# Two output projections that keep finished rows on chip, and four loads and stores in other places

## What is computed

```python
def layer_output(x, branches, w_out):          # end of each layer
    mixed = jnp.concatenate(branches, axis=-1) # branches, each times silu(gate)
    return x + mixed @ w_out                   # output projection and residual
# layer 0: dilated attention and retention, layer_output, giving x1
# layer 1: rmsnorm(x1) @ w_in (2864 columns), sparse attention, layer_output, giving x2
# result:  rmsnorm(x2) * final gain, for the prompt and for the samples
```

## Time and profile before

| what | value |
|---|---|
| three runs | 2055.37, 2053.42 and 2056.6 us, median 2055.37 |
| the profiled execution | 2053.46 us, span 2051.2 us, mean granted clock of TensorE 0.966 |
| PE | 1893.7 us busy, 92% of the span, 13566 matmuls |
| PE's weight load | 1455.8 us, 71% |
| DVE, ACT, POOL | 855.3, 699.1 and 507.2 us: 42%, 34%, 25% |
| DMA | 261.58 MB, mean 128 GB/s |
| chain that ended last | from 1910.78 us; DMA 2%, PE 2% and DVE 1% of the span |

### The profile page before, as it was taken

How to read it: one execution, slowest core, us unless ns; L and a number is a source line. 1 busy time by engine, 2 the same in 40 slices (tenths; PEclk the granted TensorE clock), 3 DMA queues, 4 the chain that set the end, 5 groups by cost and what they waited for, 6 DMA issues and landing times. The chain is left out here.

```text
span 2051.2 us, 35233 instructions
## 1 busy us (share of the span) xinstructions
PE 1893.7 (92%) x13566; PEld 1455.8 (71%) x13566; DVE 855.3 (42%) x2503; ACT 699.1 (34%) x1527; POOL 507.2 (25%) x628
## 2 busy tenths in 40 slices
PE   7999998997895898999969999999899999999695
PEld 6777776676663887878867555554688887888695
DVE  5222221774443424221411221212677777777433
ACT  5100000663332223000002322232577767667412
POOL 0000000796542000000004212110365555555000
PEclk9999999998996999999989999999999999999998
DMA  5444432655577754644336241332400000000565
GB/s 204 154 141 146 143 140 93 194 162 155 181 224 206 253 190 133 209 144 156 114 76 246 82 165 47 140 98 59 119 23 22 15 15 22 23 12 32 185 198 181
DMA packets 163171, 261.58 MB, mean 128 GB/s; under 512 B 33890, under 2 KB 113440, under 8 KB 158656
## 3 DMA queue, kind: packets, MB, share of 16 engines
q1 hardware_dynamic: 144976, 212.73, 32.7%
q0 software_dynamic: 4608, 33.56, 4.5%
q10 hardware_dynamic: 13424, 13.05, 2.5%
HBM read 210.57 MB, written 55.77 MB: 130 GB/s over the span
## 5 line engine op out<-in xcount | busy, mean ns | idle before, releaser
L1619 POOL TENSOR_SCALAR sparse_pr<-sparse_pr,sparse_coef,sparse_gate 128x63 f32<-128x63 f32 (+8 forms) x384 | 246.0, 658 | 208.0 <-DVE sparse_coef L1575 208.0
L1001 PE MATMUL x_acc<-x_w_hi,x_y_lo 128*128 128x478 f32 (+3 forms) x768 | 274.7, 358 | 1.9 <-DVE x_y_lo L855 1.6
L1001 PE MATMUL x_acc<-x_w_lo,x_y_hi 128*128 128x478 f32 (+3 forms) x768 | 269.2, 351 | 0.0
L1001 PE MATMUL x_acc<-x_w_hi,x_y_hi 128*128 128x478 f32 (+3 forms) x768 | 268.6, 350 | 0.0
L2656 PE MATMUL ss_ps_h<-ss_xT,cmp_w 128*128 128x508 f32 x512 | 244.0, 594 | 0.8 <-ACT ss_xT L2494 0.8
L1520 ACT ACTIVATE sparse_pr<-sparse_pr,sparse_nmax 128x63 f32<-128x63 f32 (+8 forms) x384 | 227.4, 597 | 2.7 <-DVE sparse_nmax L1569 2.7
L1621 POOL TENSOR_SCALAR dilated_pr<-dilated_pr,dilated_coef 128x1024 f32<-128x1024 f32 (+7 forms) x64 | 109.0, 1722 | 372.3 <-DVE dilated_coef L1575 372.3
L445 PE MATMUL h_acc<-h_w_hi,h_y_lo 128*128 128x512 f32 x448 | 177.3, 396 | 0.8 <-DVE h_y_lo L370 0.8
L445 PE MATMUL h_acc<-h_w_hi,h_y_hi 128*128 128x512 f32 x448 | 174.7, 390 | 0.0
L445 PE MATMUL h_acc<-h_w_lo,h_y_hi 128*128 128x512 f32 x448 | 174.6, 390 | 0.0
L1001 PEld LDWEIGHTS x_acc<-x_w_hi,x_y_lo 128*128 128x128 f32 x768 | 146.0, 190 | 29.4 <-issue 14.7
(11 more groups left out here) (353 smaller groups left out, 2780.5 us busy)
## 6 DMA issues: line engine op xcount, KB each, us to landing
h<-h_out SPq DMA_DIRECT2D x56, 256.0 KB, 2.1
h_w_side<-in_even_w_in SPq DMA_DIRECT2D x16, 896.0 KB, 5.0
h_w_raw<-in_even_w_in SPq DMA_DIRECT2D x6, 2048.0 KB, 8.0
x_w_side<-in_odd_w_in SPq DMA_DIRECT2D x16, 716.0 KB, 4.8
x_w_raw<-in_odd_w_in SPq DMA_DIRECT2D x5, 1912.0 KB, 8.5
h<-x_out SPq DMA_DIRECT2D x40, 239.0 KB, 2.2
ev_unit<-in_cache_a_k SPq DMA_DIRECT2D x4, 2048.0 KB, 8.9
ev_unit<-in_cache_a_v SPq DMA_DIRECT2D x4, 2048.0 KB, 11.1
```

The costliest lines, as they stand in the source:

```text
L1001: last = nc.tensor.matmul(acc[b][:, 0:passes[p][3]], left[:, k, t * P:(t + 1) * P], weights(right, p)[:, k, :], start=(k == 0 and a == 0), ...
L1619: nc.gpsimd.tensor_scalar(row, row, one, gate[:, t, 2 * i + e, (br + 1) % 3:(br + 1) % 3 + 1], ALU.mult, ALU.mult).then_inc(scaled, 1)
```

## The change

- **Rows kept.** In both projections the products of passes 0 and 1 of some tiles stay in SBUF (`held`): all eight tiles in the last projection, tiles 0 to 3 in the first. They are neither stored nor read back; the last 340 columns are added to the same row. In the first projection their whole rows (512 KB) are stored once, when complete. The memory comes from tiles that are idle then: `cmp_w1` in the first, keys, pieces and raw constants of the sparse phase in the last. `cmp_lent` (16 KB a partition) now serves in turn as raw weights of the first projection, the prompt's keys and values, the samples' turned keys, the prompt's turned keys, and gain, side outputs and a scratch row of the last projection.
- **Squares** of the last projection go to a scratch row; the wait for the store of the tile two before moves from ACT's square to DVE's scaling.
- **Samples of the last projection.** All eight side steps run in pass 1, one a tile. Their rows are read back at the start of the third pass, squared after tile 3, scaled after tile 4 and stored at tile 5.
- **Last quad.** The sixteen stores move from the end of `rest_of_even` into the first projection's pass 0, four behind the load of each of tiles 2 to 5; SP waits for them ahead of the samples' rows.
- **Prompt's keys and values** for the MLP are loaded on SP at the start of the first projection's last pass instead of on ACT in the sample phase.
- **Page table.** Constants are loaded first, then half the table on SP and half on ACT.
- Two phases become one, and a third (`rounds`) encloses them: one more barrier at the very end.

```diff
-    step_at = {NT + 2 * s: s for s in range(KD)}
+    step_at = {NT + (2 if norm_to is None else 1) * s: s for s in range(KD)}
...
-        w_raw = sb("w_raw", [P, KD, widest]) if early is None else early.w_raw
+        if early is None:
+            w_raw = comp.lent[:, 0:KD * widest].rearrange("p (k c) -> p k c", k=KD)
+        else:
+            w_raw = early.w_raw
...
+            held = [comp.w1[0][:, 4 * t:4 * t + 4, :].rearrange("p l f -> p (l f)") for t in range(4)]
...
+            w_side, outb, res, held, junk = early.w_side, None, early.res, early.held, early.junk
...
+        def leaves(n):
+            return n // NT > last_out or n // NT < last_out and n % NT >= len(held)
+
         def stored_count(p, t):
-            return 16 * evacuations(number(p, t))
+            n = number(p, t)
+            return 16 * sum(1 for m in range(n + 1) if m % 3 == n % 3 and leaves(m))
+
+        def kept_count(t):
+            return 16 * sum(1 for m in range(len(held), t + 1) if m % 2 == t % 2)
+
+        def row_of(t):
+            return held[t] if t < len(held) else x[:, t % 2, :]
...
-                    if t < 2:
+                    if t < len(held):
+                        return
+                    if t - 2 < len(held):
                         sp.wait_ge(turned[0], NT // 2 + 1)
                         sp.wait_ge(turned[1], NT // 2)
                     else:
                         rb, ru = turn_of(t - 2, True)
                         sp.wait_ge(rows_ready[rb], ru + 1)
-                        if norm_to is None:
-                            sp.wait_ge(completed_stored[b], 16 * (t // 2))
+                        sp.wait_ge(completed_stored[b], 16 * (t // 2))
                     for p in range(last_out):
...
+                    if not leaves(number(p, t)):
+                        return
...
-                    sp.dma_start(dst[0][place(t), KEPT:D], x[:, t % 2, KEPT:D]).then_inc(completed_stored[t % 2], 16)
+                    c0 = 0 if t < len(held) else KEPT
+                    sp.dma_start(dst[0][place(t), c0:D], row_of(t)[:, c0:D]).then_inc(completed_stored[t % 2], 16)
...
+                    if quad is not None and t == NT:
+                        quad.wait_stored(sp)
                     load_gated(t, n)
+                    if quad is not None and t < 6:
+                        quad.store_last(sp, t - 2)
...
-                        load_kept(0)
-                        load_kept(1)
+                        for t in range(len(held), min(len(held) + 2, NT)):
+                            load_kept(t)
+                        if norm_to is not None:
+                            load_sample_rows()
                     if p == first_next:
                         load_sample_rows()
                     if p == first_next + 1 and comp is not None:
                         load_compressor()
+                    if p == n_passes - 1 and comp is not None:
+                        sp.wait_ge(w_cut, n_passes - 1)
+                        for pp in range(first_next, n_passes - 1):
+                            if columns(pp).start < VC + P and KC < columns(pp).stop:
+                                for t in range(NT):
+                                    sp.wait_ge(stored[out_buffer(pp, t)[0]], stored_count(pp, t))
+                        comp.load_prompt(sp, dst_next[0])
...
+                        if p == last_out and norm_to is not None and t == 5:
+                            sp.wait_ge(sample_ready, 1)
+                            sp.dma_start(norm_to[1], x[0:NS, 1, :]).then_inc(sample_stored, 16)
+                        if p == last_out and len(held) <= t < NT - 2:
                             load_kept(t + 2)
                 if norm_to is not None:
-                    load_sample_rows()
                     store_normed(NT - 1, P)
...
-                    act.wait_ge(kept_in[b], 16 * (u + 1))
-                    rb, ru = turn_of(t, True)
-                    if norm_to is not None:
-                        if t >= 2:
-                            act.wait_ge(normed_stored[b], 16 * u)
-                    elif t >= 2:
+                    if t >= len(held):
+                        act.wait_ge(kept_in[b], kept_count(t))
+                    if norm_to is None and t >= 2:
                         pb, pu = turn_of(t - 2, True)
                         act.wait_ge(turned[pb], pu + 1)
-                    nc.scalar.activation(z[0:n, b, :], x[0:n, b, :], ACT.Square, accum_out=stat[0:n, b, 0:1]).then_inc(squares[b], 1)
+                    if norm_to is not None and t >= 2:
+                        act.wait_ge(inverses[b], u)
+                    to = z[0:n, b, :] if norm_to is None else junk[0:n, :]
+                    nc.scalar.activation(to, row_of(t)[0:n, :], ACT.Square, accum_out=stat[0:n, b, 0:1]).then_inc(squares[b], 1)
...
+                def square_sample_rows():
+                    act.wait_ge(kept_in[0], 16)
+                    nc.scalar.activation(x[0:NS, 1, :], x[0:NS, 0, :], ACT.Square, accum_out=stat[0:NS, 2, 0:1]).then_inc(sample_squared, 1)
+                    act.wait_ge(sample_squared, 1)
+                    nc.scalar.activation(stat[0:NS, 2, 2:3], stat[0:NS, 2, 0:1], ACT.Sqrt, scale=1.0 / D, bias=eps[0:NS, 0:1]).then_inc(sample_root, 1)
...
+                            if norm_to is not None and t == 3:
+                                square_sample_rows()
...
-                if norm_to is not None:
-                    square_rows(NT, NS)
...
+                    if norm_to is not None and t >= 2:
+                        dve.wait_ge(normed_stored[b], 16 * u)
+                    nc.vector.scalar_tensor_tensor(out=z[0:n, b, :], in0=row_of(t)[0:n, :], scalar=stat[0:n, b, 3:4],
                                                    in1=g[0:n, :], op0=ALU.mult, op1=ALU.mult).then_inc(rows_ready[turn_of(t, True)[0]], 1)
...
-                        dve.wait_ge(kept_in[t % 2], 16 * (t // 2 + 1))
-                        nc.vector.tensor_tensor(x[:, t % 2, KEPT:D], acc[b][:, 0:width], res[:, b, 0:width], ALU.add).then_inc(completed[t % 2], 1)
+                        if t >= len(held):
+                            dve.wait_ge(kept_in[t % 2], kept_count(t))
+                        nc.vector.tensor_tensor(row_of(t)[:, KEPT:D], acc[b][:, 0:width], res[:, b, 0:width], ALU.add).then_inc(completed[t % 2], 1)
                         return
                     so_far = stored_count(p, t) - 16
+                    if not leaves(number(p, t)):
+                        dve.wait_ge(res_in[b], 16 * (u + 1))
+                        nc.vector.tensor_tensor(held[t][:, columns(p)], acc[b][:, 0:width], res[:, b, 0:width], ALU.add).then_inc(evacuated[b], 1)
+                        return
...
+                            if norm_to is not None and t == 4:
+                                norm_sample_rows()
...
+        self.held = [ks_in[:, t * D:(t + 1) * D] for t in range(4)] + [c_in[0][:, t * D:(t + 1) * D] for t in range(2)]
+        self.held += [x[:, D:2 * D] for x in pieces]
+        self.junk = comp.lent[:, D + 512:2 * D + 512]
...
-            kT_all = sb("kT_all", [P, 2, 2, T])
+            kT_all = out_loads.lent[:, :].rearrange("p (m g c) -> p m g c", m=2, g=2)
...
+    def store(self, sp, q, a):
+        for j in range(NJ):
+            at = a * 32 + j * 8
+            sp.dma_start(self.mix_s[(4 * q + a) * NJ + j, 0:512].rearrange("(h d) -> h d", d=HD),
+                         self.rows[at:at + 8, :]).then_inc(self.stored, 16)
+
+    def store_last(self, sp, a):
+        self.store(sp, NB // 4 - 1, a)
+
+    def wait_stored(self, sp):
+        sp.wait_ge(self.stored, 16 * NB * NJ)
...
-            def store_quad(q):
-                sp.wait_ge(d_ready, q + 1)
-                for a in range(4):
-                    for j in range(NJ):
-                        at = a * 32 + j * 8
-                        sp.dma_start(mix[T + (4 * q + a) * NJ + j, 0:512].rearrange("(h d) -> h d", d=HD),
-                                     o_d[at:at + 8, :]).then_inc(d_stored, 16)
-            store_quad(0)
+            sp.wait_ge(d_ready, 1)
+            for a in range(4):
+                quad.store(sp, 0, a)
             for hh in range(BH - 2, BH):
                 nb, nu = bank("state", hh)
                 sp.wait_ge(bank_free[nb], nu + 1)
             for e in range(2):
                 for m in range(NB // 2):
                     sp.dma_start(state_s[2 * m + e].rearrange("h k v -> k h v"), st_s[e * HD:(e + 1) * HD, m, :, :]).then_inc(s_stored, 16)
-            store_quad(1)
             sp.wait_ge(s_stored, 16 * (NB + 1))
-            sp.wait_ge(d_stored, 16 * 16 * QUADS)
...
+        self.lent = ctx.enter_context(nc.sbuf_tensor("cmp_lent", [P, 2 * PAST], F32))
+        self.p_loaded = ctx.semaphore("cmp_p_loaded")
+        self.x_p = [self.lent[0:NPC, m * PAST:(m + 1) * PAST].rearrange("p (g s d) -> p g s d", g=2, s=16) for m in range(2)]
+
+    def load_prompt(self, sp, h_p):
```

(25 more changed lines are left out.)

86 lines of the change are left out of this document (53 added, 33 removed).

## The result

Four executions of the changed kernel took 2019.49 us in the median (2015.07 to 2021.36), the kernel before beside them 2055.18 (2053.42 to 2056.6, four executions): a ratio of 0.983, 95% interval 0.9817 to 0.9843. The gain is 35.7 us where 41.4 were forecast, and the time lies within the range of 2003 to 2024. The profiled execution took 2015.07 us, span 2012.95, and was the fastest of the four; against the profile of before its span is 38.3 us shorter.

What follows compares the result with a forecast made beforehand. PE is busy for 92% of the span, so only its gaps can be taken: -6.2 - 1 - 2 - 11 - 10 - 11.1 = -41.3 us, span 2009.9, execution 2012.2, plus 1.9 for the median: 2014 us, range 2003 to 2024.

Steps and rivals of the forecast that it cites:

- part 1: Border from even phase to first projection: without the last quad's stores the next phase opens at 638.5, -6.2 us (-5.3 to -7.2).
- The split of the 1.82 us by halves: End of the even phase: of 1.82 us landing plus barrier, some 0.9 us were taken to remain as barrier.
- part 2: Opening passes without stores of kept tiles: -2 us in the last projection (0 to -4), -1 in the first (+1 to -3).
- part 3: First projection's third output pass: fewer read-backs, transposition of tile 5 at 777.3 instead of 788.25, -11 us (-7 to -14).
- The first rival: Read-back of tiles 6 and 7 and the gather become a second limit: 2024 us, chance 0.2.
- The slower rival: Last pass of the first projection: the prompt's loads block SP ahead of all stores, 2064 us at 15 us each; chance 0.02.
- part 4: Start of the sample phase: PE no longer waits for four loads and the gather starts sooner, -10 us (-5 to -12.5).
- far bound: Largest gain allowed for a term; at the start of the sample phase it was -12.5 us.
- The lower bound of -5: Start of the sample phase: the gather gains nothing, PE waits from 1089.0 to 1090.3, and later pieces come late.
- The DMA share of 1.42: DMA engines during 1066 to 1070, sample phase: read as issue alone not being the limit, and as support for a late gather.
- The hope of 2.5 us from the clock: Sample phase: PE's gap shrinks from 13.7 to 3.9 us, so its low clock may give back up to 2.5 us.
- part 5: Last projection's last pass and end: no read-back chain, samples normed early, end at 2040.1, -11.1 us (-9 to -13).

## Why the prediction was right, and where it was not

**The last quad (part 1).** -6.45 us against -6.2. The split of the 1.82 us by halves was nearly right (0.9 taken, 0.74 measured), and the waits of the later loads hide the sixteen DMAs, as the kernel with the stores back showed.

**Opening passes (part 2).** In the last projection -1.8 us against -2. The ten profiles that keep rows there have 42.1 to 43.6 us, the kernel with no rows kept 44.93, and the kernel before 45.37 and 44.1. In the first projection the profile gives -3.1 against -1, but this term can't be told from the execution: the same code gives 44.04 and 47.76 us. The four executions of the change lie from 2015.07 to 2021.36 us; the profiled one is of the short kind and the fastest, which is why the profiles differ by more (38.3 us) than the medians (35.7). That the slower executions are of the long kind is likely and not shown, as only one execution of each set is profiled.

**Third output pass (part 3).** 40.46 us to the transposition of tile 5. The pass began at 788.25 - 51.24 = 737.0 before, so the working of the prediction gives 777.3 - 737.0 = 40.3. It named what is late next (the cut of the next weights), and cutting it in pieces took away the wait. The first rival's read-back of tile 7 shows as a wait of DVE of 1.60 us and costs PE nothing. The slower rival did not come either: the prompt's four loads are issued on SP at 997.52 within 3.64 us, and the passes around them are no longer than before.

**The sample phase (part 4): the failed step.** "PE can then start at 1063.3: -9.9 us" holds for the first eight transpositions only. The step left out the consumer: PE's banks are emptied by DVE, and in DVE's program the row numbers, which wait for table and constants, stand ahead of those copies. The bounds of the part asked what else PE needs and looked at the gather, which had room to spare. The trace of before shows the trap, in two rows of DVE and one of PE that I had not read:

```profile
1075.13 0.17 DVE L2879 CAST ss_pages_f<-ss_pages 128x8 f32<-128x8 int32 x1 [11.29 <-DMA constants_ss<-in_const]
...
1075.69 0.75 DVE L2886 COPY ss_pselT<-ss_ps_t 128x256 f32<-128x256 f32 x2
...
1076.16 3.52 PE L2314 MATMUL ss_ps_t<-constants_shared,ss_ksT 64*128 64x64 f32 x24 [1.89 <-DVE ss_pselT L2886]
```

DVE got its constants at 1075.13, 2 us after PE had its data, and PE then waited for DVE. With DVE's wait as it was, taking PE's own DMA wait away could bring nothing. What did come is what DVE got sooner: it went on 11.94 us after the opening before and 7.76 after, 4.2 us, of which 3.1 came with the loads gone from here and 1.0 with the table split. The gather, which was put at 6 us sooner, gained the same 4.2 (12.89 to 8.70 us after the opening). From there to the MLP it is 4.48 us in both, and the last 0.8 us fell in the MLP. With DVE's order turned the part gives 35.77 - 23.0 = -12.8 us, a little beyond its far bound. The lower bound of -5 was met, but by luck: it stood for a late gather, and PE never waited for a piece. The rule of the Trainium skill (DMA: Bandwidth & Descriptors, Issuing engines are not separate DMA queues) that spoke for it was borne out in size (1.0 us for the split) without being the cause. The DMA share of 1.42 that the prediction set beside it shows busy DMA engines and not whose transfers; the kernel with the table as before is what bears on it. The hope of 2.5 us from the clock was in vain: the MLP takes 17.0 and 16.5 us in the two profiles of before, 16.20 with the change after the wait of 7.66, and 16.32 where there is none.

**The end (part 5).** -12.7 us against -11.1. Up to the issue of the last store all is as worked out: 3.6 us. The mis-sized term is what follows the issue: 5.0 for the landing and 1.7 for the rounds of barrier, 6.7 us, and it is 5.04 in all. The landing takes 2.6 us and the rounds the other 2.4. The 4.3 us that the landing was worked out from is the median of all eight stores of before; the last full one, at 2044.56, landed in 2.6 there as well. The takes are 3.71 us apart and not the forecast 4.1, since the side steps that shared this pass now run in pass 1; the last product comes no sooner by it. Of the 12.7, the kernel with the samples at the end shows 8.5 for the rows kept (91.40 to 82.92) and 4.2 for the samples' place. In the one that keeps no rows the samples' place saved 3.4 us at the very end and lost more than that by the later read-backs. The side weights didn't stop PE in pass 1.

**Untouched code.** +1.2 us before the projection and +2.2 in the sparse part were in no term of the sum. Thirteen profiles of the same even phase end it between 633.7 and 640.0 us. The -1.3 us in the rest of the third pass is of this kind too: it is the clock behind the wait of 3.14 us, and four profiles with the same code there have 30.4 to 31.6 us, no less than the 30.1 and 30.3 of the kernel before.

So the failed part 4 (5.0 short) and the untouched stretches (3.4) outweigh the better end (1.6), the opening pass (2.1) and the rest of the third pass (1.3) and next passes (0.5): -41.3 + 5.0 + 3.4 - 1.6 - 2.1 - 1.3 - 0.5 = -38.4, the measured -38.3 but for rounding and the smaller terms. That the total came as near as it did is in part luck: errors of over 8 us one way met some 5.5 us the other way, and of the latter the opening pass and the rest of the third pass belong to the executions profiled. One slip of the sum: the near bounds of the parts add to -25.3 us, not -26.

## What to carry to other kernels

When a load is moved off an engine's path, follow its result one engine further: whoever empties the buffer that the engine fills has a program of its own, and a wait that stands there ahead of the emptying takes the place of the one removed. Work that waits on a DMA goes behind work that waits on nothing outside, as long as its own consumer has the time. The landing of a store is best read from the store that stands in the same place, not from a median over the program. Compare two profiles stretch by stretch, and profile the old kernel twice before a difference of some us in code that nobody touched is explained.

## What the runs showed of the hardware

- The same code has stretches of two lengths in different executions: the opening pass of the first projection 44.04 or 47.76 us, the stretch of sparse attention 199.8 or 201.9. In the first the difference is a longer wait for one load (3.73 against 1.66 us) and matmuls at the lower level of the clock behind it.
- The same wait of PE can cost clock or not: behind a wait of 3.14 us, before which PE had been at the upper level, the granted clock stayed at 1.00 in three profiles and was 0.91 to 0.94 over the rest of the pass in four, 1.5 to 2.7 us more for the same matmuls.
- Constants of the sample phase reached DVE 5.3 us after their issue where four DMAs of 256-byte pieces were issued on ACT at the phase's opening, and 3.2 us where these were not there: 2.1 us in the landing, against 0.8 us in the sixteen issues of the table.
- A last DMA of 512 KB, the end of its phase and that of the enclosing one fit into 5.04 us after the issue: 2.6 us for the landing, 2.4 for the two ends.
